# Residual gates as rows through device memory, and the keys and queries of the differential attention turned by VectorE, in a kernel of two transformer stacks on one Trainium2 core

## The reference, cut to what the change touches

Two blocks of two layers each run one behind the other on 256 tokens of width 1024. The change touches the first block only: there a context stream and a latent stream go through the same projection, three branches (retention, differential attention, a small gated MLP), a merge, and a gated residual. `gate` is one row of 1024 numbers for all tokens; in the latent stream the keys and queries of the differential attention are rotated.

## Time and profile before

| | |
|---|---|
| median of 3 runs | 1780.93 us (1780.88 to 1781.08) |
| the profiled execution | 1780.77 us |
| span of its trace, first to last instruction | 1778.8 us |
| granted clock of PE in it (share of full speed) | 0.999 |
| first block / second block in the span | to about 925 us / from there |

### The profile page before, as it was taken

How to read it: one execution, slowest core, us unless ns; L and a number is a source line. 1 busy time by engine, 2 the same in 40 slices (tenths; PEclk the granted TensorE clock), 3 DMA queues, 4 the chain that set the end, 5 groups by cost and what they waited for, 6 DMA issues and landing times.

```text
span 1778.8 us, 25433 instructions
## 1 busy us (share of the span) xinstructions
PE 1760.9 (99%) x9055; PEld 1471.4 (83%) x9055; DVE 876.2 (49%) x1782; ACT 1025.6 (58%) x1513; POOL 1363.4 (77%) x573
## 2 busy tenths in 40 slices
PE   7999999999999999999999999999999999999998
PEld 4888888888888888888888878898888887888887
DVE  2785544845744546375337974321112985432112
ACT  4645675445577654466665567555555576745554
POOL 5867787866778878677869865888887965678886
PEclk9999999999999999999999999999999999999999
DMA  9975656754566667455647644556665754466663
GB/s 367 314 242 156 176 174 206 233 168 143 154 182 186 178 208 241 131 158 161 191 136 221 177 131 132 176 176 191 189 189 172 203 157 129 139 189 190 189 189 129
DMA packets 171554, 327.87 MB, mean 184 GB/s; under 512 B 10432, under 2 KB 16064, under 8 KB 171456
## 3 DMA queue, kind: packets, MB, share of 16 engines
q1 hardware_dynamic: 168272, 320.22, 58.6%
q10 hardware_dynamic: 3184, 6.32, 1.0%
HBM read 325.46 MB, written 1.05 MB: 184 GB/s over the span
## 4 chain that ended last, share of the span: by engine, by line
PE 69%; POOL 15%; issue 14%; DMA 1%; ACT 0%; POOLq 0%; DVE 0%; SPq 0%; DVEq 0%; ACTq 0%
PE G L1941 16%; PE G L1943 16%; PE G L1942 16%; POOL wlo L528 15%; PE A L2636 3%; PE G L2636 3%; PE A L1941 2%; PE A L1943 2%; PE A L1942 2%; PE A L2637 1%; PE G L2637 1%; PE A L2410 1%; PE G L2425 1%; DMA raw<-in_w_in 1%; PE A L1995 1%
## 5 line engine op out<-in xcount | busy, mean ns | idle before, releaser
L528 POOL TENSOR_TENSOR wlo<-raw,whi 128x1024 fp32r<-128x1024 f32 (+1 forms) x568 | 1359.7, 2406 | 401.9 <-ACT whi L553 398.4
L553 ACT ACTIVATE whi<-raw 128x1024 fp32r<-128x1024 f32 (+1 forms) x568 | 593.5, 1048 | 570.9 <-PE G L1943 432.3
L1941 PE MATMUL G<-whi,hparts 128*128 128x512 f32 (+1 forms) x1472 | 578.8, 393 | 1.0 <-DVE hparts L1285 0.6
L1943 PE MATMUL G<-whi,hparts 128*128 128x512 f32 (+1 forms) x1472 | 567.8, 386 | 0.0
L1942 PE MATMUL G<-wlo,hparts 128*128 128x512 f32 (+1 forms) x1472 | 567.4, 385 | 0.0
L1941 PEld LDWEIGHTS G<-whi,hparts 128*128 128x128 f32 x1472 | 276.4, 188 | 59.9 <-issue 6.5
L1943 PEld LDWEIGHTS G<-whi,hparts 128*128 128x128 f32 x1472 | 276.3, 188 | 56.3
L1942 PEld LDWEIGHTS G<-wlo,hparts 128*128 128x128 f32 x1472 | 276.7, 188 | 52.0
L1866 DVE TENSOR_TENSOR G<-G,frelu 128x512 f32<-128x512 f32 x12 | 8.4, 699 | 188.9 <-ACT frelu L1125 188.9
L1692 DVE STREAM_TRANSPOSE t<-z 32x256 f32<-32x256 f32 (+2 forms) x256 | 96.8, 378 | 3.8
L1941 PE MATMUL G<-whi,osplit 128*128 128x512 f32 x240 | 94.2, 393 | 0.0
(11 more groups left out here) (430 smaller groups left out, 2501.1 us busy)
## 6 DMA issues: line engine op xcount, KB each, us to landing
raw<-in_w_in SPq DMA_DIRECT2D x324, 512.0 KB, 3.8
raw<-in_w_up SPq DMA_DIRECT2D x64, 512.0 KB, 3.7
raw<-in_w_down SPq DMA_DIRECT2D x64, 512.0 KB, 3.3
raw<-in_w_out SPq DMA_DIRECT2D x40, 512.0 KB, 3.9
raw<-in_w_branch_out SPq DMA_DIRECT2D x36, 512.0 KB, 4.2
modw<-in_w_mod SPq DMA_DIRECT2D x32, 512.0 KB, 5.4
raw<-in_w_branch SPq DMA_DIRECT2D x24, 512.0 KB, 3.3
modz<-in_w_mod SPq DMA_DIRECT2D x16, 512.0 KB, 9.8
```

The source lines that it names most:

```text
L528: pool.tensor_tensor(wlo[:, s, :, 0:n], raw[:, s, :, 0:n], whi[:, s, :, 0:n].bitcast(F32), ALU.subtract)\
L553: act.activation(whi[:, slot, :, 0:n], raw[:, slot, :, 0:n], ACT.Copy).then_inc(hi_ready, 1)
L1941: pe.matmul(bank, hi, whi[:, slot, kk, 0:n], start=first, stop=False)
L1943: return pe.matmul(bank, lo, whi[:, slot, kk, 0:n], start=False, stop=last)
```

```diff
+        gate_row = sb_at("gate_row", [P, D], F32, place["aT"])
...
-        modG = sb("modG", [P, DEPTH, KT, 2])
+        modG = sb("modG", [P, DEPTH, 2, KT])
+        gateT = sb("gateT", [DEPTH * 2 * KT, P])
+        gate_dram = nc.dram_tensor("gate_rows", (DEPTH, 2, D), F32, kind="Internal").ap()
...
+        DEALT = (0, 10, 19, 27, 32)
+        GATE_STORE = 9
...
+                        if n in (0, 3) and c == GATE_STORE:
+                            sp.wait_ge(gate_turned, w(gate_turned))
+                            sp.dma_start(gate_dram[l].rearrange("a (k p) -> (a k) p", p=P), gateT[2 * KT * l:2 * KT * (l + 1), :])\
+                              .then_inc(gate_stored, 16)
...
-                    for c in range(D // CH):
-                        act.wait_ge(gate_spread, w(gate_spread))
-                        act.activation(gate_row[:, c * CH:(c + 1) * CH], A[c][:], ACT.Copy).then_inc(gate_copied, 1)
...
-                    evacuate(1, columns(z, DV) if is_x else ctx_values, ACT.Copy, beside=beside_dv)
+                    evacuate(1, columns(z, DV) if is_x else ctx_values, ACT.Copy, beside=None if is_x else beside_dv)
...
+                act.wait_ge(gate_stored, w(gate_stored, 16) if n != 1 else w(gate_stored, 0))
+                act.dma_start(gate_row[:], gate_dram[l, 0 if is_x else 1].partition_broadcast(P)).then_inc(gate_in, 16)
...
+                for q in range(P // PART):
+                    part = slice(q * PART, (q + 1) * PART)
+                    ins = dve.transpose(gateT[:, part], modG[part].rearrange("p l a k -> p (l a k)"))
+                ins.then_inc(gate_turned, 1)
...
-            def residual(src):
-
+            def residual(src, splits):
+
+                dve.wait_ge(gate_in, w(gate_in, 16))
+                dve.wait_ge(h_split, splits)
                 for c in range(D // CH):
-                    dve.wait_ge(gate_spread, w(gate_spread))
                     cols = slice(c * CH, (c + 1) * CH)
-                    link(dve.tensor_tensor(A[2 + c][:], oproj[:, 0, cols], A[c][:], ALU.mult))
-                    ins = dve.tensor_tensor(A[c][:], oproj[:, 1, cols], A[c][:], ALU.mult)
+                    dve.tensor_tensor(A[2 + c][:], oproj[:, 0, cols], gate_row[:, cols], ALU.mult)
+                    ins = dve.tensor_tensor(A[c][:], oproj[:, 1, cols], gate_row[:, cols], ALU.mult)
...
+            dve.memset(modG[:], 0.0)
...
-                            dve.tensor_tensor(s1, x1, sin, ALU.mult)
-                            link(dve.tensor_tensor(s2, x2, sin, ALU.mult))
-                            dve.tensor_tensor(x1, x1, cos, ALU.mult)
-                            link(dve.tensor_tensor(x2, x2, cos, ALU.mult))
+                            factor = DH ** -0.5 if c == 3 else 1.0
+                            dve.scalar_tensor_tensor(s1, x1, factor, sin, ALU.mult, ALU.mult)
+                            link(dve.scalar_tensor_tensor(s2, x2, factor, sin, ALU.mult, ALU.mult))
+                            dve.scalar_tensor_tensor(x1, x1, factor, cos, ALU.mult, ALU.mult)
+                            link(dve.scalar_tensor_tensor(x2, x2, factor, cos, ALU.mult, ALU.mult))
...
+                def turn_diff_heads(part):
+
+                    for m in range(DEALT[part], DEALT[part + 1]):
+                        a, col = ((2, DKc), (3, DQ))[m // 16]
+                        rows, feats = (slice(q * PART, (q + 1) * PART) for q in divmod(m % 16, 4))
+                        ins = dve.transpose(tT[feats, a].rearrange("p h (t s) -> p t h s", t=TT)[:, :, :, rows],
+                                            z[rows, :, col:col + W].rearrange("p t (h f) -> p t h f", f=P)[:, :, :, feats])
+                    if part == H1 - 1:
+                        ins.then_inc(diff_heads, 1)
...
+                    if is_x and i < H1:
+                        turn_diff_heads(i)
...
-                if gate is not None:
-                    for c in range(D // CH):
-                        for b in range(CH // P):
-                            ins = pe.matmul(A[c][:, b * P:(b + 1) * P], gate[:, c * (CH // P) + b].to_broadcast([P, P]), ident,
-                                            start=True, stop=True)
-                        ins.then_inc(gate_spread, 1)
...
-                    if c == 3:
+                    if c == 3 and not is_x:
                         for g in ((4,), (5,), (6, 7), ())[s]:
                             head_group(g)
...
+                if is_x:
+                    pe.wait_ge(diff_heads, w(diff_heads))
```

More of the change, by code:

```diff
@@ L322, in build @@
         mod_used, mod_copied = sem("mod_used"), sem("mod_copied")
-        gate_ready = sem("gate_ready")
+        gate_ready, gate_turned, gate_stored, gate_in = (sem(n) for n in ("gate_ready", "gate_turned", "gate_stored", "gate_in"))
         modw_used, rows_turned, rows_summed = sem("modw_used"), sem("rows_turned"), sem("rows_summed")
-        gate_copied, squared = sem("gate_copied"), sem("squared")
+        squared = sem("squared")
         raw_full = [sem(f"raw_full{i}") for i in range(SLOTS)]
@@ L351, in build @@
         mlp_vn, mlp_mixed = sem("mlp_vn"), sem("mlp_mixed")
+        diff_heads = sem("diff_heads")
         branches_ready = sem("branches_ready")
@@ L354, in build @@
         split_turned, split_hi, split_lo = sem("split_turned"), sem("split_hi"), sem("split_lo")
-        branch_out, merged, gate_spread = sem("branch_out"), sem("merged"), sem("gate_spread")
+        branch_out, merged = sem("branch_out"), sem("merged")
         idx_dots, idx_relu, idx_summed = (sem(n) for n in ("idx_dots", "idx_relu", "idx_summed"))
@@ L1249, in gate_rows @@
             def gate_rows(c, l):
-                link(dve.tensor_tensor(modG[:, l], mod_rows(c, 2), bmodT[:, l, 2 * KT:].unsqueeze(2).to_broadcast([P, KT, 2]), ALU.add))
-                return dve.tensor_tensor(modG[:, l], modG[:, l], gpostT[:, l].unsqueeze(2).to_broadcast([P, KT, 2]), ALU.mult)
+                own = modG[:, l].rearrange("p a k -> p k a")
+                link(dve.tensor_tensor(own, mod_rows(c, 2), bmodT[:, l, 2 * KT:].unsqueeze(2).to_broadcast([P, KT, 2]), ALU.add))
+                dve.tensor_tensor(own, own, gpostT[:, l].unsqueeze(2).to_broadcast([P, KT, 2]), ALU.mult).then_inc(gate_ready, 1)
+                dve.wait_ge(gate_ready, w(gate_ready))
+                for q in range(P // PART):
+                    part = slice(q * PART, (q + 1) * PART)
+                    ins = dve.transpose(gateT[:, part], modG[part].rearrange("p l a k -> p (l a k)"))
+                ins.then_inc(gate_turned, 1)
             def first_shift_scale(half):
@@ L1465, in _ @@
                 if n == 1:
-                    residual(cx)
+                    residual(cx, 2 * SLOTS)
                 if n == 3:
@@ L1493, in _ @@
                 if n == 2:
-                    residual(x)
+                    residual(x, 3 * SLOTS)
                     decays((0,), l)
@@ L1511, in _ @@
                     sum_rows(1)
-                    gate_rows(0, l).then_inc(gate_ready, 1)
-                    dve.wait_ge(gate_ready, w(gate_ready))
+                    gate_rows(0, l)
                 dve.wait_ge(evacuated, w(evacuated, 2 * TT if n < 3 else 0))
@@ L1546, in _ @@
                         sum_rows(7)
-                        gate_rows(6, 1).then_inc(gate_ready, 1)
-                        dve.wait_ge(gate_ready, w(gate_ready))
+                        gate_rows(6, 1)
                     dve.wait_ge(evacuated, w(evacuated, 2 * TT))
@@ L2216, in branch, with merge @@
                         ins.then_inc(weights_used, 1)
-            def merge(ready, y, gate=None, late_bank=False, first=0, edge=None, turn=None):
+            def merge(ready, y, late_bank=False, first=0, edge=None, turn=None):
                 for u in range(first, 6):
@@ L2448, in _ @@
                 merge(out_projected if n == 3 else projected, lambda t, k: z[:, t, Y_HOMES[k // 4] + k % 4 * P:Y_HOMES[k // 4] + (k % 4 + 1) * P],
-                      modG[:, l, :, 0:1] if is_x else modG[:, l, :, 1:2], True,
+                      True,
                       edge=(lambda: turn_tokens(normed, HB_EDGE, (0, 1))) if n < 2 else None, turn=turn_first_tile if n == 3 else None)
```

5 lines of the change are left out of this document (removed).

## The result

The changed kernel takes 1771.81 us (median of 5 runs, 1771.74 to 1772.16), the kernel before 1780.93 beside it (1780.76 to 1781.08): a ratio of 0.9948, with a 95% interval of 0.9937 to 0.9958. It is faster by 9.1 us. The profiled execution took 1771.81, of which the span is 1769.9.

What follows compares the result with a forecast made beforehand. PE's own work was taken to set the time in the first block's passes. The terms -5.3 - 4.0 + 0.2 = -9.1 us against the profiled 1780.77 gave 1771.7 us, range 1770.6 to 1776.5.

Steps and rivals of the forecast that it cites:

- part 2: Beside the slabs of DV in passes 1 and 3, PE's transposes of latent keys and queries go: -4.0 us.
- part 4: Residual's four products, now reading two SBUF tensors, may wait for POOL's low parts: +0.2 us, bounds 0 and 4.9.
- Part 1: In passes 0, 1 and 3 PE no longer spreads the gate over 128 rows, 1.78 us each: -5.3 us.
- Part 3: VectorE does 32 transposes a pass over the retention steps, 14 us, hidden with 3.4 us of cover.
- Part 5: The gate's way through memory, with four small transposes, a store and a load of 512 KB: hidden, 0 us.
- The supply: Rival: the load of 512 KB delays the weight slabs by 3.4 us in three passes: +10.2, 1781.9 us; chance 0.08.
- the contended turns: Rival: VectorE's transposes contend with POOL, PE waits 45 us in each of two passes: near 1862 us; chance 0.03.
- The first rival: Residual products wait for POOL all four times at both places: +4.9 instead of +0.2, 1776.4 us; chance 0.07.

Runs made afterwards that it cites:

- The kernel with that part alone: Kernel before, with the gates sent through memory but the latent keys and queries still turned by PE: 1775.60 us, 0.9967 of the kernel before.
- the run with 1.3 us: Changed kernel with four turns of the keys made once more in pass 1 ahead of the modulation sums: 1773.54 us.
- those with 3.3 and more: Changed kernel with eight turns repeated in pass 1: 1777.11 us; all 32 turns dealt to the fourth retention step: 1794.41; pass 1's residual products made twice: 1783.05.

## Why the prediction was right

The forecast was 1771.7, the time 1771.8. The mechanism held, but two terms were off, part 2 by 0.26 us and part 4 by 0.2 the other way, and cancel: that the number fits to 0.1 us is luck.

- **Part 1** held: -5.3 forecast, three steps of 1.78 in both kernels that have it. The kernel with that part alone is 5.3 us under the first runs of the kernel before, 5.5 under those beside it.
- **Part 2** was mis-sized: -4.0 forecast, -3.74 measured. The step that failed is the reading of the earlier trace rows, which sets every slab of DV against a plain one of 2.72. But a slab behind a group of transposes is longer by 0.10 to 0.14, and the groups of RV and of the modulation rows stay. In pass 1 the first slab was to come down to 3.52 with its eight transposes and takes 3.65 (2.86 without them); the next two were to come down to 5.44 and take 5.54. The slab behind them gave 0.10 that was not counted. That makes 1.87 us for 2.00, and pass 3 gave 1.87 too. The foot of the range allowed for change-overs priced too low, so for more gain; this one went the other way.
- **Part 3** held: hidden, the turns at 436 ns, the cover 3.45 for 3.4. The weights of the second step came at 393.89 with PE's stream 3.6 us earlier, so 3.7 us later beside that stream (3.5 forecast), and PE did not wait. One price was wrong: the rotation as scalar_tensor_tensor takes 416 ns (median of 16 products from a bank), as the plain forms of that rotation do (414), not 475; the row I took reads its scalar from a tile, where the rotation has a constant (whether that is the reason was not tried). So 0.4 us a column was counted that isn't there. (Its working, 16 x 4 x 0.05, is 3.2 and not 1.6; a pass has 32 such products, and 32 x 0.05 is the 1.6 that was used.) The price of a missed cover was wrong as well: "each us of lateness would be a us of PE" holds for the wait of 1.3 us, not for 3.3 (5.1) or 8.5 (11.2).
- **Part 4** was the doubtful term, +0.2 with bounds of 0 and 4.9, and measured 0. Its working held: two products caught in pass 1 and none in pass 2, RK's rotation 4.35 us late for 4.1 forecast, then 1.96 and 1.5 behind the idle places, and 1.51 at the sums. With the 0.4 us a column left out, its own chain gives 4.1 - 2.43 - 0.49 = 1.2 against a cover of 1.8, and no wait. The cover left is 0.25 us, so the term was near its edge. The cover of RK's rotation was 6.4 us and not 5.3: in the kernel before PE begins the slab that needs it at 328.27, and the rotation ends near 321.9. The bound of 4.9 takes a wait of 2.5 there, where 8.3 less 5.3 is 3.0; with 6.4 it is 1.9.
- **Part 5** held: the four small transposes are 0.20 us each, 0.84 with their issue for 0.9. The load took 4.7 us for the 3.4 of the earlier trace rows; nobody noticed, not even at three times the size.
- **The rivals.** The supply is out by the kernel with three loads, the contended turns by 64 at 445 ns or less. The first rival, all products caught, is the right mechanism: six in a row were caught while POOL ran without a pause. It did not come at these places because POOL rested when the first two products began in pass 1, and all four in pass 2 (the last at 589.90, POOL's next low part at 590.25). Its price counts a us of waiting as a us, which the run with 1.3 us bears out and those with 3.3 and more do not; its own waits of some 2.5 lie between, and no run shows them.

## What to carry to other kernels

Where one engine is busy for 99% of the span, work moved off it is worth what two slabs of the same surroundings differ by, not what its instructions last. Read the room for it on the other engine between its last instruction and the moment the busy engine asks for the result, place by place: the idle time shown there includes the busy engine's own answer, and the busy engine comes earlier by all that it has saved ahead of the place. Price a missed cover above its length where it is long (3.3 us and more here), since such a wait of PE brought its clock down. And when anything moves, look where the products of two SBUF tensors now begin: one that slipped behind the start of a low part took up to 2.9 us for 0.7.

## What I had not expected of the hardware

- A wait of PE costs more than itself when it is long: 1.3 us cost 1.5, with the clock at 1.00 throughout; 3.3 cost 5.1, 8.5 cost 11.2 (twice) and 9.1 cost 11.0, with granted clocks of 0.50 to 0.64 for some 4 us or more behind the wait.
- The exclusion is felt on both sides: POOL's low parts, 2.4 us alone, took 2.65 to 2.86 beside the products. And it isn't confined to products of two SBUF tensors: two of the tensor_scalar in the row, at 95.79 and 99.00 in the kernel before, took 2.51 us where those beside them took 0.28, each over a whole low part.
- A slab behind a group of transposes takes 0.10 to 0.14 us longer than one behind a slab.
